# Outputs and residual between the units of the w1 products, and one w2 unit of the first expert kept in memory of its own

## The reference, cut to what matters

```python
logits = xf @ router_w + router_b
top_val, top_idx = top_k(logits, 4);  gates = softmax(top_val)      # 32 experts
for each expert e, for the tokens that chose it:
    hcat  = x @ w1[e] + b1[e]                                       # 1024 -> 2048
    x_glu = min(hcat[:, ::2], 7);  x_lin = clip(hcat[:, 1::2], -7, 7)
    g     = x_glu * sigmoid(1.702 * x_glu) * (x_lin + 1)
    y    += gate * (g @ w2[e] + b2[e])                              # 1024 -> 1024
h = h + y;  out = RMSNorm_final(h)
```

## Time and profile before

| | us |
|---|---|
| median of 3 runs | 1273.55 (1270.11 to 1274.01) |
| the profiled execution | 1271.14 |
| its span | 1269.3 |
| busy: PE / DVE / ACT / POOL | 1226.6 / 373.5 / 239.3 / 49.2 |
| first product with w1 starts at | 341.8 |
| weights of the experts | 192 units of 2 MB |

### The profile page before, as it was taken

One profiled execution on the slowest core, in us unless ns is written; L12 is line 12 of the kernel. 1 busy time (PEld: TensorE's weight loads), 2 busy tenths in 40 slices (PEclk: granted clock), 3 DMA queues, 4 the chain that ended last, 5 costly groups with the idle time before them and its releaser, 6 DMA issues.

```text
span 1269.3 us, 14609 instructions
## 1 busy us (share of the span) xinstructions
PE 1226.6 (97%) x5732; PEld 520.7 (41%) x5732; DVE 373.5 (29%) x756; ACT 239.3 (19%) x487; POOL 49.2 (4%) x46
## 2 busy tenths in 40 slices
PE   8999999999999999999999999999999999999997
PEld 6766666544433333333333333333333333333322
DVE  2468432775330221213032221213031221212122
ACT  2014343534201111120111112020111111110103
POOL 0000031512000000000000000000000000000000
PEclk9999999999999999999999999999999999999999
DMA  9697679249799999999999999999999999999994
GB/s 282 230 325 261 244 266 345 93 152 347 286 429 415 429 429 429 428 429 429 428 428 429 428 430 429 428 429 428 428 429 429 429 429 429 428 428 428 428 428 196
DMA packets 67439, 476.21 MB, mean 375 GB/s; under 512 B 7704, under 2 KB 25396, under 8 KB 40428
## 3 DMA queue, kind: packets, MB, share of 16 engines
q1 hardware_dynamic: 65278, 471.87, 90.7%
q10 hardware_dynamic: 1582, 2.03, 0.5%
q0 software_dynamic: 544, 1.84, 0.4%
HBM read 468.47 MB, written 7.24 MB: 375 GB/s over the span
## 4 chain that ended last, share of the span: by engine, by line
PE 75%; DMA 20%; DVE 2%; ACT 2%; issue 1%; SPq 0%; DVEq 0%; ACTq 0%
PE ps L2252 28%; DMA ring<-in_w 19%; PE ps L2274 11%; PE ps L1751 10%; PE ps L2198 4%; PE ps L2053 4%; PE ps L2190 2%; PE ps L2185 2%; PE ps L1794 1%; PE ps L2187 1%; PE ps L2240 1%; PE ps L2260 1%; PE ps L1976 1%; PE ps L1770 1%; PE ps L2093 1%
## 5 line engine op out<-in xcount | busy, mean ns | idle before, releaser
L2252 PE MATMUL ps<-ring,own 128*64 128x512 f32 x1536 | 340.2, 593 | 12.5 <-DMA ring<-in_w 12.5
L2252 PEld LDWEIGHTS ps<-ring,own 128*64 128x64 f32 x1536 | 111.8, 137 | 227.0 <-issue 194.8
L1625 DVE TENSOR_SCALAR own<-ps 128x512 f32<-128x512 f32 x32 | 22.1, 692 | 533.0 <-PE ps L2252 533.0
L2274 PE MATMUL ps<-ring,own 128*64 128x512 f32 x768 | 171.3, 594 | 4.6 <-ACT own L1053 4.6
L1751 PE MATMUL ps<-own,ring 128*128 128x288 f32 x512 | 131.8, 411 | 1.4 <-DVE own L1128 1.1
L2252 PE MATMUL ps<-own 128*64 128x512 f32 x512 | 115.9, 592 | 2.3 <-DMA own<-in_w 2.3
L1751 PEld LDWEIGHTS ps<-own,ring 128*128 128x128 f32 x512 | 95.7, 191 | 31.9 <-issue 3.3
L2274 PEld LDWEIGHTS ps<-ring,own 128*64 128x64 f32 x768 | 56.1, 137 | 111.3 <-issue 111.3
L2198 PE MATMUL ps<-own 128*128 128x512 f32 x180 | 88.5, 617 | 0.0
L1059 ACT ACTIVATE own<-ps 64x512 f32<-64x512 f32 x64 | 37.9, 592 | 222.9 <-PE ps L2274 222.1
L1616 DVE TENSOR_TENSOR own<-ps,own 128x512 f32<-128x512 f32 x34 | 21.9, 686 | 172.5 <-PE ps L2206 172.5
(11 more groups left out here) (361 smaller groups left out, 979.0 us busy)
## 6 DMA issues: line engine op xcount, KB each, us to landing
ring<-in_w SPq DMA_DIRECT2D x143, 2048.0 KB, 29.5
own<-in_w SPq DMA_DIRECT2D x48, 2048.0 KB, 28.1
ring<-in_w_in SPq DMA_DIRECT2D x16, 1024.0 KB, 6.2
ring<-in_cache_win_k SPq DMA_DIRECT2D x16, 1024.0 KB, 6.5
ring<-in_cache_win_v SPq DMA_DIRECT2D x16, 1024.0 KB, 8.9
ring<-in_w_out SPq DMA_DIRECT2D x6, 1024.0 KB, 11.1
ring<-in_state_ssm SPq DMA_DIRECT2D x8, 512.0 KB, 10.9
out_ssm_sample<-ring SPq DMA_DIRECT2D x8, 512.0 KB, 9.6
```

Of the source, the lines that this page charges most:

```text
L1625: nc.vector.tensor_scalar(xg_o, hid[:, 0], LIMIT, None, ALU.min).then_inc(sem("glu_ready"), 1)
L2252: last = nc.tensor.matmul(ps[C * half:C * half + C, 1 + m, :], xT[:, k, C * u:C * u + C], rows[:, D * half + 512 * m:D * half + 512 * m + ...
L2274: last = nc.tensor.matmul(ps[C * half:C * half + C, 4, :], gT[:, (k % 4) * P + C * (k // 4):(k % 4) * P + C * (k // 4) + C], rows[:, 512 * ...
```

## The change

- The combine and the three transposes of the gate matrix (`outputs_before`) are issued inside `hidden(pt, 0)`, ahead of k = 4; expert 1's `hidden` follows directly on expert 0's.
- In the closing pair, `residual(0)` stands ahead of k = 2 and `residual(1)` ahead of k = 4 of expert 1; tile 1 is added up in banks 3 and 5 and tile 2 in 1 and 2.
- VectorE adds the outputs and builds the selections ahead of `gated_units(pt, 0)`; ScalarE copies GT ahead of the sigmoid.
- The inputs times the norm's weights (`xT`) move from VectorE (two instructions) to ScalarE (eight, `input_columns`), between gT's copy and the output rows of expert 1.
- Unit 8 of the first eight experts' turn (the first w2 unit of expert 0) is loaded once into a place of its own, `resident`, issued on SP behind the last of the mixer's loads before the wait for `M_ready`; the load of unit 8 in the stream is left out, with the counts of place 0 set back by one load. Unit 16 still waits until unit 8 has been used.
- The first turn of four experts is written out ahead of the loop over turns.
- The program's DMA scratch is set to 1024 bytes, and `own` grows from 28500 to 32200 words a partition.

```diff
+RESIDENT = 2 * W1_UNITS
...
-        WORDS = 28500
+        WORDS = 32200
...
+        resident = take(2 * SLOT)
...
-        FINAL_BANKS = (slice(6, 8), slice(1, 3), slice(3, 6, 2))
+        FINAL_BANKS = (slice(6, 8), slice(3, 6, 2), slice(1, 3))
...
+            sp.dma_start(resident, a["w2"][0].rearrange("e (s p o) c -> e s p (o c)", p=P, o=W2_ROWS)[0, 0]).then_inc(sem("resident_full"), 16)
             sp.wait_ge(sem("M_ready"), len(BATCHES))
...
-            for n in [3, 0, 4, 2, 1] + list(range(5, PER_EXPERT * TURN)):
+            for n in [3, 0, 4, 2, 1] + [n for n in range(5, PER_EXPERT * TURN) if n != RESIDENT]:
...
+            def input_columns(gathers):
+
+                for half in range(2):
+                    act.wait_ge(sem("xT_ps"), 2 * gathers - 1 + half)
+                    for j in range(4):
+                        last = nc.scalar.activation(xT[:, 4 * half + j, :], ps[:, 3 + 2 * half, j * P:(j + 1) * P], ACT.Copy,
+                                                    scale=vecs[:, 28 + 4 * half + j:29 + 4 * half + j])
+                    last.then_inc(sem("xT_ready"), 1)
...
-                sigmoid(2 * pt)
                 act.wait_ge(sem("GT_ps"), pt + 2)
                 nc.scalar.activation(GT, ps[:, 0, 0:TOK], ACT.Copy).then_inc(sem("GT_ready"), 1)
+                sigmoid(2 * pt)
...
                 hidden_columns(2 * pt + 1)
+                if not ending:
+                    input_columns(pt + 2)
                 expert_rows(pt, 1)
...
+                if u:
+                    dve.wait_ge(sem("g_ready"), et)
...
-                    gated_units(pt, 0)
                     dve.wait_ge(sem("comb_read"), 4 * pt + 4)
                     add_outputs(2 * pt)
...
                     build_selections(2 * pair + 2, pt)
+                    gated_units(pt, 0)
                     gated_units(pt, 1)
                     build_b1_rows(2 * pair + 2)
-                    expert_inputs(pt + 2)
...
+                    u = n % UNITS
+                    if opening and n == RESIDENT:
+                        pe.wait_ge(sem("resident_full"), 16)
+                        return
+                    kept = 16 if u == RESIDENT % UNITS and not (opening and n < RESIDENT) else 0
+                    pe.wait_ge(unit_full(u), turns + (16 * (n // UNITS + 1) + unit_base(u) - kept))
...
-                    hidden(pt, 0, first, {})
...
+                    hidden(pt, 0, first, {4: outputs_before})
...
-                    hidden(pt, 1, first, {4: tile_0} if closing else {})
+                    hidden(pt, 1, first, {2: tile_0, 4: tile_1} if closing else {})
...
-            with pe.Fori(0, turns_before_last) as t:
-                expert_turn(t, False)
-            expert_turn(turns_before_last, True)
+            expert_turn(0, True, False)
+            with pe.Fori(1, turns_before_last) as t:
+                expert_turn(t, False, False)
+            expert_turn(turns_before_last, False, True)
...
-    nc = bacc.Bacc("TRN2", target_bir_lowering=False, num_devices=1)
+    nc = bacc.Bacc("TRN2", target_bir_lowering=False, num_devices=1, dynamic_dma_scratch_size=1024)
```

More of the change, by code:

```diff
@@ L2222, in residual, with expert_turn @@
                 n = ROWS[c]
-                banks = (6, 7) if c == 0 else (1, 2) if c == 1 else (3, 5)
+                banks = (6, 7) if c == 0 else (3, 5) if c == 1 else (1, 2)
                 for half in range(2):
                     nc.tensor.matmul(ps[0:n, banks[half], :], ident[0:n, 0:n], h[0:n, c, 512 * half:512 * half + 512], start=True, stop=False)
-            def expert_turn(t, ending):
+            def expert_turn(t, opening, ending):
                 turns = t * (16 * (PER_EXPERT * TURN // UNITS))
                 def wait_unit(n):
-                    pe.wait_ge(unit_full(n % UNITS), turns + (16 * (n // UNITS + 1) + unit_base(n % UNITS)))
+                    u = n % UNITS
[4 more added lines that the diff above has]
+                    pe.wait_ge(unit_full(u), turns + (16 * (n // UNITS + 1) + unit_base(u) - kept))
                 def hidden(pt, u, first, between):
@@ L2271, in second @@
                             pe.wait_ge(sem("end_rows"), 16)
-                        rows = d3(unit(n % UNITS), D)[:, k % W2_ROWS]
+                        rows = d3(resident if opening and n == RESIDENT else unit(n % UNITS), D)[:, k % W2_ROWS]
                         for half in range(2):
@@ L2283, in expert_turn, with outputs_before @@
                     pe.wait_ge(sem("sel_ready"), pt + 1)
-                    hidden(pt, 0, first, {})
[L2286 to L2296, removed]
+                    def outputs_before():
+                        pe.wait_ge(sem("GT_ready"), pt + 1)
+                        pe.wait_ge(sem("ysb_ready"), 4 * pt + 1)
+                        pe.wait_ge(sem("comb_read"), 4 * pt + 4)
+                        combine()
+                        pe.wait_ge(sem("S_ready"), 4 * pt + HEAD_SELECTIONS)
+                        for c in range(3):
+                            n = ROWS[c]
+                            last = nc.tensor.transpose(ps[:, 0, cols(c)], S2[0:n, c, :], ident[0:n, 0:n])
+                        last.then_inc(sem("GT_ps"), 1)
+                    hidden(pt, 0, first, {4: outputs_before})
                     def tile_0():
@@ L2300, in tile_0, with tile_1 @@
                         residual(0)
-                    hidden(pt, 1, first, {4: tile_0} if closing else {})
+                    def tile_1():
+                        pe.wait_ge(sem("comb_read"), 4 * pt + 8)
+                        residual(1)
+                    hidden(pt, 1, first, {2: tile_0, 4: tile_1} if closing else {})
                     pe.wait_ge(sem("comb_read"), 4 * pt + 8)
@@ L2309, in expert_turn @@
                         gather()
-                    else:
-                        pe.wait_ge(sem("hid_read"), 2 * pt + 3)
-                        residual(1)
                     second(pt, 0, first)
@@ L2316, in expert_turn @@
                     if closing:
-                        pe.wait_ge(sem("xT_ready"), 2 * pt + 4)
+                        pe.wait_ge(sem("hid_read"), 2 * pt + 3)
                     hidden_turn(pt, 1)
```

## The result

| | before | after |
|---|---|---|
| median of 9 runs each, us | 1270.11 (1268.03 to 1274.01) | 1278.58 (1275.20 to 1282.38) |
| ratio, 95% interval | | 1.0057 [1.0041, 1.0073] |
| profiled execution: time / span | 1271.14 / 1269.3 | 1282.25 / 1279.4 |
| first w1 product (pair 0) starts at | 341.82 | 344.63 |
| from there to the end of the span | 927.5 | 934.8 |

The profiled execution after is among the longer of its nine. 2.8 us of its difference lie ahead of the first product, and they are there 17 us into the span: the first input landed 0.9 us later, and the granted clock of the first 32 us was 0.84 against 0.95 before. The change does nothing there. It is 7.3 us longer, 0.57% of the whole, as the timed ratio.

The account below looks back on a forecast made before the run. TensorE bound eight pairs at 56.16 us, then DMA at 58.72. With pairs of 57.71 us and a closing 68.24, span 1275.7, time 1277.5, plus 0.5: 1278.0 us; own range 1274.5 to 1282, 8 in 10 for 1271 to 1283.

Parts of the forecast that it names:

- The limits before, 56.16 and 58.72 us a pair: In the MoE before: TensorE-bound at 56.16 us a pair for eight pairs, DMA-bound at 58.72 after them.
- +1.55 us a pair: Each pair: insertion 5.39, wait for VectorE's reads 1.37 and bias 0.56, less the old insertion's 5.77; pair becomes 57.71 us.
- The closing pair: Last pair, residuals moved earlier: 0 within 0.1 us, a gain only where the run waits for data; 68.24 us to the end.
- The stream binds no more: Weight stream: closest at pair 14's last w1 unit, landed 1175.6, needed 1181.2; TensorE comes 5.6 us later.
- The resident unit is worth nothing: Unit 8 kept aside: 4.9 us less transfer, mostly given back by a later stream; its load costs nothing.
- 1.8 to 2.4 us later: Stream from unit 10 on: 2.4 us later than before, less up to 0.6 for a dip, not 4.9 earlier.
- Beside other work: VectorE's additions and selections hidden with 4 us to spare; eight ScalarE copies, 2.3 us, and the sigmoid cost nothing.
- Rival A: MoE end: the stream still binds, the closing pair profits, kernel faster; span 1266.9, time 1268.7 us; chance 0.11.
- Rival C: Sixteen waits of 1.4 us drop the clock to 1.2 GHz, 3.4 us each, 54 us in all; time 1332; chance 0.02.
- The split of a w1 run: w1 matmuls around the insertion: splitting costs 0.18 us a pair (7.05 against 6.87), though the skill would make it free.

Follow-up runs that it names:

- e2: The kernel before with the resident unit, smaller scratch and opening turn written out, but the outputs where they were; ratio 0.9998 to the kernel before.
- e3: e2 with the free place filled at once: unit 16 issued behind the use of unit 0, ahead of unit 9; ratio 0.9987 to the kernel before.
- e4: The changed kernel with expert 1's products in banks 3 and 4 instead of 1 and 2; ratio 0.9996 to the kernel before.
- e1: The changed kernel without its resident unit, the scratch at its old size; ratio 1.0052 to the kernel before.
- e5: e4 without the resident unit, the scratch at its old size; ratio 0.9995 to the kernel before.
- e6: e4 with e3's order of loads, and in pair 0 alone the outputs behind the first expert; ratio 0.9991 to the kernel before.
- e9: e6 with pair 0's outputs ahead of k = 6 of the first expert; ratio 0.9982 to the kernel before.
- e8: The changed kernel with one more VectorE instruction (0.6 us) ahead of its two reads of expert 0's products; ratio 1.0172 to the kernel before.
- e7: The kernel before with the DMA scratch of 1024 bytes and nothing else; ratio 1.0005 to the kernel before.

## Why the prediction was right, point by point

- **The limits before, 56.16 and 58.72 us a pair.** Right. e2, e3 and e4 show the same two regimes, with the change's parts in and out.
- **+1.55 us a pair.** The pairs after are (1211.02 - 344.63) / 15 = 57.76 us apart, +1.60. The insertion was 5.21 + 0.17 as predicted. The wait with the bias rows was 1.99 against 1.93: after a stop the bias matmuls are not 0.56 but 0.62 long. 0.05 x 15 = 0.8 us is nearly all that the sum missed.
- **The closing pair.** From its first product to the end 1279.4 - 1211.02 = 68.4 us, predicted 68.24. That this part gains only where the run waits for data was right, and here it never did.
- **The stream binds no more.** Right: no wait for DMA in the w1 products. The sum gave 6.4 us, the stretch 7.3, and the medians differ by 8.5, the ratio by 0.57%. That the forecast of 1278.0 lies 0.6 us from the measured median is luck: it stood for 4.5 us above the median of three runs, and the median of nine is 3.4 us lower than that.
- **The resident unit is worth nothing.** Right in the changed kernel: e1 against after, e5 against e4. "1.8 to 2.4 us later" was measured as 1.6 to 1.7 us up to pair 12 in e4 and e5, and as 2.2 in pair 14 of e5. Its load itself cost nothing either: it was over by 240 us (437 GB/s from 230 to 235, 95 from 235 to 240, then 0 to 1).
- **Beside other work.** VectorE stood idle for 4.27 us before expert 0's reads in pair 1, predicted 4. The eight ScalarE copies took 2.17 us, predicted 2.3; they end 5.6 us ahead of the next pair's first product at 402.34, and TensorE didn't wait for them:

```profile
394.61 2.17 ACT L1045 ACTIVATE own<-ps,own 128x128 f32<-128x128 f32 x8
401.94 0.59 ACT L1071 ACTIVATE own<-ps 64x512 f32<-64x512 f32 x1 [5.15 <-PE ps L2294]
```

- **Rival A was priced wrong.** e4 is its case, the wait away and the stream binding, and it took the time of the kernel before and not 2.4 us less (within 0.2%, so a part of the 2.4 could hide in the interval). The step that failed is "the last half unit would land at 1253.6, a quarter of a w2 run follows": behind the last landing for which it waits, TensorE alone has 93.5 us to do (e5). The 16 landings that are left take 16 x 4.893 = 78.3 us, and 1.8 and 11.5 us follow them by rival A's own numbers: 91.6, which is less. I had priced the stream's end and not TensorE's way to it. In e6 and e9, where TensorE came to the closing pair earlier, a wait did show there, at a unit that landed 1.3 and 1.1 us behind the stream's pace (the step told under e4).
- **Rival C** falls at 1.39 us, and e8 shows how close it was: at 1.99 us the clock did fall, in 4 of 16 pairs. It was overpriced as well: a fall cost 1.7 us each time and not 3.4, as the clock came back within the group. The section of the Trainium skill that the prediction named ("TensorE: Matmul & The Clock Gate", "HAM oscillation") has longer waits than any of these in its example; the one behind it, "A second HAM failure mode: psum-queue depth-cycling", is the nearer one: in it frequent short idle times between groups of matmuls make the clock go down and up. The waits of 1.99 us agree with that; those of 1.39 us, as frequent, brought no fall.
- **The split of a w1 run.** By the rule of the Trainium skill in "TensorE: Matmul & The Clock Gate", Part 2, it would cost nothing; 32 instructions took 7.04 behind the insertion and 6.87 ahead of it (7.02 in e4, where no wait follows), so here the row with the 0.18 held.

## What to carry to other kernels

Before moving work out from between two uses of the same banks, look up what it was hiding: here 5 us of matmuls lay over 1.3 us of reads, and the kernel's own last pair showed the naked wait. When two limits are 5% apart, count in which stretch each binds and how much lead is left: TensorE gained 2.6 us a pair on the stream before, and met it in pair 9; with 1.6 us more a pair it gained 1.0 and didn't meet it in 16 pairs. And a prefetched unit is worth its transfer only if the places behind it come free in time: follow the queue until it is steady, since in e3 it ran dry half a pair later.

## What the runs showed of the hardware that was not expected

- A wait of TensorE of 1.39 us, 16 times in an execution, left the granted clock at 1.00 in the windows shown, and every pair at 57.70 to 57.85 us. One of 1.99 us in the same place let it fall to 1.2 GHz for a while in 4 of 16 pairs, 1.7 us each. Of three single waits for the stream, 2.12 us (e4) and 2.44 us (e2) were followed by such a fall and 2.17 us (e5) was not, so the length of the wait alone doesn't decide it.
- In seven of the eight profiles in which TensorE waits for the stream (all but e7) one landing in pairs 13 to 15 came 0.5 to 1.6 us later than the pace of those ahead of it says, at an even rate. The cause is open. A step of this size is as large as most of the differences between e2 and e9.
- With a DMA scratch of 1024 bytes GpSimd's six DMAs, three of them with 512 KB, were issued as fast as with the default (0.52 to 0.86 us).
- The first 32 us ran at a granted clock of 0.84 in one profiled execution and 0.95 in another, and the first w1 product came 2.8 us later in the first. The clock alone doesn't set this: at 0.84 too, it came at 343.16 in e7 and at 342.63 in e8, 1.3 and 0.8 us later than before. Over all eleven profiles it lies between 340.06 and 346.03. In a kernel of 1270 us that is 0.5%, more than most of the parts under study; measuring from the first product onward took it out.
